# Retention with tokens as the stationary operand for v and the input norm applied behind the matmuls, and the first two units of two FFNs taken side by side

## The chip, the core and the metric

One core of one Trainium2 chip runs the whole program, a chain of eight phases over one sequence of 512 tokens. The metric is the device time of one execution in microseconds. The time before is the median of 3 runs.

## The reference, cut to what matters

x has 512 rows of 1024 numbers, all in float32. The first two of the eight phases are these (the fourth is the second one again with other weights):

```python
def retention(xn, w_in, w_out):              # xn = rms_norm(x, a_norm_pre)
    q, k, v, g = split(xn @ w_in)            # 1024 | 1024 | 2048 | 2048 columns, 4 heads
    q, k = rotary(q), rotary(k) * dk ** -0.5
    ...                                      # causal, with a decay per head:
    out = (q @ k.T * decay) @ v              # per head 512 x 512
    out = rms_norm(out)                      # over the 512 columns of a head
    return (silu(g) * out) @ w_out

def conv_ffn(xn, w_up, conv_w, conv_b, w_down):   # xn = rms_norm(x, gain)
    h = xn @ w_up                            # 1024 -> 5632
    hc = causal depthwise convolution of h, width 3
    g, u = split(hc)
    return (silu(g) * u) @ w_down
```

After each phase x = x + rms_norm(h, gain). The other phases (diff, conformer, nsa and two more FFNs) are not touched.

## The kernel before, in words

**Layout and precision.** x is kept transposed: 8 chunks of 128 features by 512 tokens. Every dense product works on split numbers: a value is a high part (`xh`, `w_hi`, rounded by a copy on ACT) and a low part (`xl`, `w_lo`, the difference). A product of a chunk is three matmuls of 512 columns: high by high, low by high, high by low (lines 720 to 722).

**A unit** is one 1024 x 128 slice of weights: 8 chunks, 24 matmuls, into one of two PSUM banks `lin`. Weights pass through two slots. SP loads `raw[s]` (line 540) as soon as the last `w_lo[s]` is made; ACT makes `w_hi[s]` (line 1266, `split`) once the slot's unit is multiplied (`unit_done`); DVE makes `w_lo[s]` (line 1819, `split_next`) and so sets `lo_done`, on which PE's unit after next waits. `bank_free` is set by whoever has read the bank. The order of work on each engine is the order in which the program is written; engines meet only at semaphores. `rounds` is a hardware loop.

**Opening.** ACT issues the DMAs for the constants, x, 37 pieces of parameters (`rows`) and `dif_lp` (lines 1768 to 1772). PE turns x into chunks (line 1206), DVE copies them to `x`, PE turns the parameters (line 1213). `norm_x` then squares each chunk on ACT (line 1274), sums over features with a matmul by ones into the bank `stat` (line 736), takes the logarithm and the exponential for the inverse rms (lines 1280 and 1282), scales x to `y` on DVE (1833), and makes `xh` on ACT (1303) and `xl` on POOL (651).

**Retention**, a loop over four heads of 12 units: two for q, two for k, four for v, four for the gate g. ACT copies each bank out (line 1366: `ret_raw`, or the silu of g into `ret_g`). DVE rotates q and k (1950 to 1954). Each 128 columns of v come out as features by tokens, so PE turns them (`turn_v`, line 773) and ACT places them (1378). Between gate units PE makes the scores (786) and, once DVE has multiplied them by the decay (1967), weighs v with them into the four banks `att` (794). ACT copies those to `ret_o` (1392), squares them, PE sums the squares (736), and DVE scales by the inverse rms and the gate (1976, 1978); `ret_hi` (1402) and `ret_lo` (1986) are the input of the last projection, `a_w_out`, in which each of 8 outputs takes two units, 16 chunks.

**ffn0 and ffn1.** The update of x before them ends on DVE chunk by chunk: y (1874), x (1877), `xl` (1838), with `xh` and a square on ACT (1288, 1274). PE's first unit takes for each chunk the sum of squares and the three matmuls, then unit 1 follows, then a loop of pairs of units. These FFNs multiply x times the gain without the rms; DVE multiplies each bank by the inverse rms `rs_x` (2400).

## Time and profile before

| | us |
|---|---|
| median of 3 runs | 3006.64 (3003.03 to 3008.56) |
| the profiled execution | 3006.15 |
| its span | 3004.3 |
| PE busy | 2822.2 (94%) |
| DVE busy | 1626.2 (54%) |
| ACT busy | 1215.4 (40%) |
| POOL busy | 192.1 (6%) |
| granted TensorE clock, mean | 0.969 |

The span runs from the first to the last instruction; the 1.85 us beside it in the execution's time lie around the program. Busy time of PE is that of pipelined matmuls whose ends are modelled, so one matmul is shown as 0.40 us where the next starts 0.23 us later. Starts are the safer reading.

### The profile page before, as it was taken

How to read it: one execution, taken by the hardware profiler on the slowest of the kernel's cores; microseconds unless marked ns; L12 is line 12 of the kernel's file. 1: busy time of each engine (PE TensorE's matmuls, PEld its weight loads, DVE VectorE, ACT ScalarE, POOL GpSimd, SP SyncE). 2: the span in 40 equal slices, each digit the busy share in tenths (PEclk: the TensorE clock that was granted, in tenths of full speed). 3: DMA queues.
4: the chain of work that ended last, by engine and by line, in shares of the span. 5: the costliest groups of instructions: out<-in, count | busy, mean ns of one | idle time of the engine just before them, and what ended most of it. 6: DMA issues, size and time to landing. Idle time of an engine off the chain costs nothing.

```text
span 3004.3 us, 34870 instructions
## 1 busy us (share of the span) xinstructions
PE 2822.2 (94%) x11902; PEld 2118.4 (71%) x11902; DVE 1626.2 (54%) x2216; ACT 1215.4 (40%) x1955; POOL 192.1 (6%) x173
## 2 busy tenths in 40 slices
PE   6999989999998998999988969999998898999999
PEld 4677757788886656888875637888876555678887
DVE  3234323777425674677436965555365667455533
ACT  3333322444324454444335654333234465443321
POOL 1000000000000000000005730000000112000000
PEclk8999989999999998999998979999998999999999
DMA  3122213233332211333331203333333000133332
GB/s 117 57 80 74 70 49 91 73 95 92 91 96 77 64 43 56 91 91 98 91 91 36 63 28 91 91 97 89 94 98 102 20 15 22 56 92 91 97 92 91
DMA packets 431346, 229.15 MB, mean 76 GB/s; under 512 B 7915, under 2 KB 427820, under 8 KB 431148
## 3 DMA queue, kind: packets, MB, share of 16 engines
q1 hardware_dynamic: 428848, 222.98, 25.5%
q10 hardware_dynamic: 2428, 5.28, 0.5%
q8 instruction: 39, 0.64, 0.1%
q14 instruction: 31, 0.25, 0.0%
HBM read 226.13 MB, written 2.10 MB: 76 GB/s over the span
## 4 chain that ended last, share of the span: by engine, by line
PE 81%; DVE 11%; ACT 4%; issue 2%; POOL 1%; ACTq 1%; DMA 0%; DVEq 0%; POOLq 0%; SPq 0%
PE lin L720 22%; PE lin L721 22%; PE lin L722 22%; DVE con_a L2238 2%; PE stat L736 2%; DVE w_lo L1819 2%; PE att L922 1%; PE lin L961 1%; PE att L794 1%; PE lin L984 1%; DVE n_sm L2147 1%; ACT w_hi L1266 1%; PE att L786 1%; PE lin L1138 1%; PE lin L1101 1%
## 5 line engine op out<-in xcount | busy, mean ns | idle before, releaser
L1819 DVE TENSOR_TENSOR w_lo<-raw,w_hi 128x1024 fp32r<-128x1024 f32 x427 | 527.6, 1236 | 775.9 <-ACT w_hi L1266 762.0
L720 PE MATMUL lin<-xh,w_hi 128*128 128x512 f32 x2048 | 830.8, 406 | 17.8 <-POOL xl L651 14.1
L721 PE MATMUL lin<-xl,w_hi 128*128 128x512 f32 x2048 | 813.7, 397 | 0.0
L722 PE MATMUL lin<-xh,w_lo 128*128 128x512 f32 x2048 | 813.4, 397 | 0.0
L1266 ACT ACTIVATE w_hi<-raw 128x1024 fp32r<-128x1024 f32 x427 | 452.1, 1059 | 665.4 <-PE lin L722 627.4
L720 PEld LDWEIGHTS lin<-xh,w_hi 128*128 128x128 f32 x2048 | 386.6, 189 | 131.5 <-issue 19.8
L721 PEld LDWEIGHTS lin<-xl,w_hi 128*128 128x128 f32 x2048 | 387.2, 189 | 97.2 <-issue 6.7
L722 PEld LDWEIGHTS lin<-xh,w_lo 128*128 128x128 f32 x2048 | 386.9, 189 | 95.0
L721 PE MATMUL lin<-ffn_lo,w_hi 128*128 128x512 f32 x704 | 279.1, 396 | 0.0
L720 PE MATMUL lin<-ffn_hi,w_hi 128*128 128x512 f32 x704 | 279.1, 396 | 0.0
L722 PE MATMUL lin<-ffn_hi,w_lo 128*128 128x512 f32 x704 | 279.1, 396 | 0.0
L720 PEld LDWEIGHTS lin<-ffn_hi,w_hi 128*128 128x128 f32 x704 | 132.6, 188 | 32.3
L722 PEld LDWEIGHTS lin<-ffn_hi,w_lo 128*128 128x128 f32 x704 | 132.6, 188 | 32.3
L721 PEld LDWEIGHTS lin<-ffn_lo,w_hi 128*128 128x128 f32 x704 | 132.6, 188 | 32.3
L1757 ACT ACTIVATE ffn_hi<-ffn_p 128x512 f32 x88 | 55.7, 633 | 218.2 <-DVE ffn_p L2423 130.5
L1755 ACT ACTIVATE ffn_s<-ffn_g 128x512 f32<-128x512 f32 x88 | 55.7, 633 | 184.2 <-DVE ffn_g L2411 184.2
L2400 DVE TENSOR_TENSOR ffn_hu<-lin,rs_x 128x512 f32<-128x512 f32 x88 | 60.8, 691 | 101.8 <-PE lin L722 101.7
L736 PE MATMUL stat<-sq,const 128*128 128x512 f32 x128 | 80.4, 751 | 36.3 <-ACT sq L1274 35.9
L657 POOL TENSOR_TENSOR x<-x,y 128x512 f32<-128x512 f32 x8 | 11.7, 1484 | 1524.2 <-DVE y L1874 1524.2
L2428 DVE TENSOR_TENSOR ffn_lo<-ffn_p,ffn_hi 128x512 f32 x88 | 60.9, 692 | 81.2 <-ACT ffn_hi L1757 81.2
L2400 DVE TENSOR_TENSOR ffn_hg<-lin,rs_x 128x512 f32<-128x512 f32 x88 | 60.9, 692 | 70.0 <-PE lin L722 40.9
L697 POOL TENSOR_SCALAR n_e<-n_e,n_sm,gates 128x128 f32<-128x128 f32 (+1 forms) x64 | 50.1, 782 | 738.5 <-DVE n_sm L2153 738.5
(328 smaller groups left out, 3562.6 us busy)
## 6 DMA issues: line engine op xcount, KB each, us to landing
raw<-in_ffn_w_up SPq DMA_DIRECT2D x176, 512.0 KB, 3.8
raw<-in_ffn_w_down SPq DMA_DIRECT2D x64, 512.0 KB, 3.7
raw<-in_a_w_in SPq DMA_DIRECT2D x48, 512.0 KB, 3.9
raw<-in_ffn_w_down SPq DMA_DIRECT2D x32, 384.0 KB, 3.2
raw<-in_conv_w_pw SPq DMA_DIRECT2D x24, 512.0 KB, 3.8
raw<-in_nsa_w_in SPq DMA_DIRECT2D x21, 512.0 KB, 3.8
raw<-in_a_w_out SPq DMA_DIRECT2D x16, 512.0 KB, 3.7
raw<-in_w_kv SPq DMA_DIRECT2D x16, 512.0 KB, 3.7
```

The costliest lines, as they stand in the source:

```text
L697: pool.tensor_scalar(n_e[:, sl, 1, 0:w], n_e[:, sl, 1, 0:w], n_inv[:, sl, 1:2], gate, ALU.mult, ALU.mult).then_inc(n_b, 1)
L720: pe.matmul(bank, w_hi[s][:, k, :], h, start=start and k == 0, stop=False)
L721: pe.matmul(bank, w_hi[s][:, k, :], l, start=False, stop=False)
L722: done = pe.matmul(bank, w_lo[s][:, k, :], h, start=False, stop=stop and k == kc - 1)
L736: pe.matmul(stat[:, :], c_("ones"), sq[(squares.n - 1) % 2][:, :], start=start, stop=stop).then_inc(sq_used, 1)
L1266: act.activation(w_hi[s][:, :, :], raw[s][:, :, :], ACT.Copy).then_inc(hi_done[s], 1)
L1755: act.activation(ffn_s[:, :], ffn_g[:, :], ACT.Silu).then_inc(f_silu, 1)
L1757: act.activation(ffn_hi[:, bass.ds(i, 1), :], ffn_p[:, :], ACT.Copy).then_inc(f_hi, 1)
L1819: dve.tensor_tensor(w_lo[s][:, :, :], raw[s][:, :, :], w_hi[s][:, :, :].bitcast(F32), ALU.subtract).then_inc(lo_done[s], 1)
L2238: done = dve.scalar_tensor_tensor(part[:, k:], att[:, 3, 0:T - k], col("conv_w_dw_2", c + j * DC), part[:, k:], ALU.mult, ALU.add)
L2400: dve.tensor_tensor(ffn_h[u][:, :], lin[b][:, :], rs_x[:, :], ALU.mult).then_inc(f_h[u], 1)
L2428: dve.tensor_tensor(ffn_lo[:, bass.ds(i, 1), :], ffn_p[:, :], ffn_hi[:, bass.ds(i, 1), :].bitcast(F32), ALU.subtract).then_inc(f_lo, 1)
```

## The change

**The norm.** a_norm_pre's gain is loaded by itself and turned into `gain_cols`. `xh` and `xl` are made from x times the gain; the inverse rms of the tokens (`ret_rs`) is applied later: to the rotation tables for q and k, to each gate bank on DVE before the silu, and to v as a scale per token (`ret_rc`, `ret_rs` turned by PE). x is loaded in two halves. PE takes the first two units side by side, chunk by chunk, with the turns of x and the sums of squares between them. The parameter rows, `ret_tab` and `dif_lp` are issued by SP behind the first two weight loads, and PE turns the parameters behind units 1 and 2.

**v.** A v unit is now 256 rows by 512 columns of weights: x's tokens are the stationary operand, the weights move, and v comes out tokens by features in `att`.

**The heads** are written out instead of looped. ACT squares `att` itself, DVE adds the squares to `acc`, and PE sums once per head. a_w_out's first product waits for one piece of `ret_lo` at a time.

**ffn0 and ffn1** take units 0 and 1 side by side, unit 1 four chunks behind; ACT splits unit 0's slot before it loads the silu table, and the first pair stands ahead of the loop.

The core of the diff, by engine:

```diff
@@ -548,10 +560,22 @@

             def retention():
...
-                            load(w_cols(w, 0, UC, h * width + (base_ + c * P)))
+                for h in range(RH):
+                    for n in range(4):
+                        load(w_cols(w, 0, UC, h * RDK + (n // 2) * RH * RDK + (n % 2) * P))
+                        if h == 0 and n == 1:
+                            for dst, src in row_dmas(a, rows):
+                                sp.dma_start(dst, src).then_inc(rows_in, 16)
+                            sp.dma_start(ret_tab[:, :], a["ret_table"]).then_inc(r_tab, 16)
+                            sp.dma_start(dif_lp, a["b_lambda"][0].rearrange("r c -> (r c)").partition_broadcast(P)).then_inc(d_lp, 16)
+                    for u in range(4):
+                        s, t = units.take()
+                        sp.wait_ge(lo_done[s], t + 1)
+                        sp.sem_inc(slot_taken, 1)
+                        sp.dma_start(broad(raw[s]), w[u * 2 * P:(u + 1) * 2 * P, 2 * RH * RDK + h * RDV:2 * RH * RDK + (h + 1) * RDV].rearrange(
+                            "(c p) n -> p c n", p=P)).then_inc(raw_full[s], 16)
+                    for c in range(RC):
+                        load(w_cols(w, 0, UC, 2 * RH * RDK + RH * RDV + h * RDV + c * P))
                 project(a["a_w_out"][0], (8, 8), DC)

```

PE:

```diff
             def retention():
-                xs = norm_x()
-                vt, vd, gs = Tally(), Tally(), Tally()
-                with rounds(pe, RH, (units, 12), (banks, 12), (squares, RC), (heads, 1), (vt, RC), (vd, RC),
-                            (r_scores, TB), (r_outs, RC)):
...
+                two = [(units.take(), banks.take()) for _ in range(2)]
...
+                for c in range(DC + 3):
+                    if 4 + c < DC:
+                        turn_x(4 + c)
+                    if c < DC:
+                        chunk(0, c)
+                        sum_square(c == 0, c == DC - 1)
+                    if c >= 3:
+                        chunk(1, c - 3)
...
+                def values(h):
+
+                    for u in range(4):
+                        s, t = units.take()
+                        pe.wait_ge(lo_done[s], t + 2)
+                        if h and u == 0:
+                            pe.wait_ge(r_og, h * RC)
+                        for c in range(2):
+                            k = 2 * u + c
+                            for b in range(TB):
+                                tok = slice(b * P, (b + 1) * P)
+                                pe.matmul(att[:, b, :], xh[:, k, tok], broad(w_hi[s])[:, c, :], start=k == 0, stop=False)
+                                pe.matmul(att[:, b, :], xl[:, k, tok], broad(w_hi[s])[:, c, :], start=False, stop=False)
+                                done = pe.matmul(att[:, b, :], xh[:, k, tok], broad(w_lo[s])[:, c, :], start=False, stop=k == DC - 1)
+                        done.then_inc(unit_done[s], 1)
...
+                for h in range(RH):
+                    if h:
+                        output(xh, xl, (UC,))
+                        output(xh, xl, (UC,))
+                    else:
+                        pe.wait_ge(rows_in, ROW_DMAS * 16)
+                        pe.wait_ge(gain_set, 1)
+                        turn_params(0, 4)
+                    output(xh, xl, (UC,))
+                    if h == 0:
+                        pe.wait_ge(par_done, 1)
+                        turn_params(4, PARAM_TILES)
+                    output(xh, xl, (UC,))
+                    if h == 0:
+                        pe.wait_ge(par_done, 2)
+                        pe.wait_ge(r_rms, 1)
...
                     output(xh, xl, (UC,))
+                    output(xh, xl, (UC,))
                     for c in range(RC):
-                        sum_square(c == 0, c == RC - 1)
-                    for c in range(RC):
-                        vd.next(), r_scores.next(), r_outs.next()
-                project(ret_hi, ret_lo, (8, 8), DC, lambda k: (r_lo, (RH * RC)))
+                        squares.next()
+                    pe.wait_ge(sq_used, squares.last())
+                    pe.matmul(stat[:, :], c_("ones"), acc[:, :], start=True, stop=True).then_inc(r_sum, 1)
+                project(ret_hi, ret_lo, (8, 8), DC, lambda k: (r_lo, k + 1))
                 sum_acc()
...
+                else:
+                    two = [(units.take(), banks.take()) for _ in range(2)]
...
+                    for c in range(DC + LAG):
+                        if c < DC:
+                            sum_square(c == 0, c == DC - 1)
+                            chunk(0, c)
+                        if c >= LAG:
+                            chunk(1, c - LAG)
...
+            pe.wait_ge(gain_in, 16)
+            pe.transpose(trp[:, 0, 0:DC], gain_rows[:, :], c_("ident")[0:DC, 0:DC]).then_inc(gain_tr, 1)
+            for c in range(4):
+                turn_x(c)
```

ACT:

```diff
             def retention(final):
-                norm_x()
-                with rounds(act, RH, (units, 12), (banks, 12), (squares, RC), (rss, 1), (heads, 1)) as i:
...
+                act.preload_act_table_set(LN)
+                for c in range(DC):
+                    act.wait_ge(x_ready, c + 1)
+                    act.activation(xh[:, c, :], x[:, c, :], ACT.Copy, scale=gain_cols[:, c:c + 1]).then_inc(xh_ready, 1)
+                    pre.next()
+                    square(x[:, c, :])
...
+                def gate(h, c):
+
+                    split_next()
+                    banks.take()
+                    act.wait_ge(r_gr, h * RC + c + 1)
+                    act.activation(ret_g[:, c, :], ret_g[:, c, :], ACT.Silu).then_inc(r_g, 1)
+
+                for h in range(RH):
+                    if h:
+                        act.wait_ge(r_pv, h * RC)
+                    raw_out(ret_raw[:, 0, :])
+                    raw_out(ret_raw[:, 1, :])
...
+                    act.wait_ge(r_rot, 2 * h + 1)
+                    raw_out(ret_raw[:, 0, :])
...
+                        split_next()
+                    s, t = multiplied()
+                    for b in range(TB):
+                        act.activation(ret_v[:, b, :], att[:, b, :], ACT.Copy, scale=ret_rc[:, b:b + 1]).then_inc(r_v, 1)
+                    split(s, t)
+                    gate(h, 0)
+                    gate(h, 1)
...
+                        act.wait_ge(r_pv, h * RC + c + 1)
+                        square(att[:, c, :])
+                    gate(h, 2)
+                    gate(h, 3)
+                    act.preload_act_table_set(LN)
...
+                    if h + 1 < RH:
+                        act.preload_act_table_set(SILU)
                     for c in range(RC):
...
+                        act.wait_ge(r_p, h * RC + c + 1)
+                        act.activation(ret_hi[:, h * RC + c, :], y[c % 2][:, :], ACT.Copy).then_inc(r_hi, 1)
+                project_out(ret_hT, 2, final, ("ffn_norm_pre", 0), table=False)
...
+                if kind == 1:
+                    split_next()
...
+                if kind == 1:
+                    pair(0, False)
+                with rounds(act, FC - (kind == 1), (units, 2), (banks, 2), (f_n, 1)) as i:
+                    pair(i + (kind == 1), True)
```

DVE (and POOL, which no longer makes xl in this phase):

```diff
+                def gate(h, c):
+
+                    b, _t = banks.take()
+                    s, t = units.n % 2, units.base + units.n // 2
+                    dve.wait_ge(unit_done[s], t + 1)
+                    dve.tensor_tensor(ret_g[:, c, :], lin[b][:, :], ret_rs[:, :], ALU.mult).then_inc(r_gr, 1)
+                    dve.wait_ge(r_gr, h * RC + c + 1)
+                    dve.sem_inc(bank_free[b], 1)
+                    split_next()
...
+                    if h == 0:
+                        dve.wait_ge(rs_ready, rss.next())
+                        dve.wait_ge(r_tab, 16)
+                        dve.tensor_tensor(cos, cos, ret_rs[:, :], ALU.mult).then_inc(r_scaled, 1)
+                        dve.tensor_tensor(sin, sin, ret_rs[:, :], ALU.mult).then_inc(r_scaled, 1)
+                        dve.wait_ge(r_scaled, 2)
+                    rotate(ret_q, 2 * h)
...
+                    for u in range(4):
+                        split_next()
+                    gate(h, 0)
+                    for j in range(TB):
+                        dve.wait_ge(r_s, h * TB + j + 1)
+                        dve.tensor_tensor(ret_s[j], att[:, j, 0:T - j * P], ret_tab[:, (2 + h) * T:(3 + h) * T - j * P], ALU.mult).then_inc(r_sd, 1)
+                    gate(h, 1)
+                    first_, second = squares.next(), squares.next()
+                    dve.wait_ge(sq_ready, second)
+                    dve.tensor_tensor(acc[:, :], sq[0][:, :], sq[1][:, :], ALU.add).then_inc(sq_used, 2)
+                    add_square()
+                    add_square()
+                    gate(h, 2)
+                    gate(h, 3)
+                    for c in range(RC):
+                        dve.wait_ge(r_g, h * RC + c + 1)
+                        dve.tensor_tensor(ret_g[:, c, :], att[:, c, :], ret_g[:, c, :], ALU.mult).then_inc(r_og, 1)
                     dve.wait_ge(rs_ready, rss.next())
-                    for _ in range(RC):
-                        squares.next()
                     for c in range(RC):
+                        dve.wait_ge(r_og, h * RC + c + 1)
                         if c >= 2:
-                            dve.wait_ge(r_lo, (h - 1) * RC + c - 1)
-                        dve.tensor_tensor(y[c % 2][:, :], ret_o[:, c, :], rs[:, :], ALU.mult).then_inc(r_p, 1)
-                        dve.wait_ge(r_p, (h - 1) * 2 * RC + 2 * c + 1)
-                        dve.tensor_tensor(y[c % 2][:, :], y[c % 2][:, :], ret_g[:, c, :], ALU.mult).then_inc(r_p, 1)
+                            dve.wait_ge(r_lo, h * RC + c - 1)
+                        dve.tensor_tensor(y[c % 2][:, :], ret_g[:, c, :], rs[:, :], ALU.mult).then_inc(r_p, 1)
                         if c:
...
+            def first_low(c):
+                dve.wait_ge(xh_ready, pre.next())
+                dve.scalar_tensor_tensor(xl[:, c, :], x[:, c, :], gain_cols[:, c:c + 1], xh[:, c, :].bitcast(F32),
+                                         ALU.mult, ALU.subtract).then_inc(xl_ready, 1)
+
             for c in range(DC):
                 dve.wait_ge(tr_done, c + 1)
                 dve.tensor_copy(x[:, c, :], att[:, c % 4, :]).then_inc(x_ready, 1)
+                if c:
+                    first_low(c - 1)
+            first_low(DC - 1)
```

The order moves at three places. The first is PE in the opening. Before (`sq` to `stat` are the sums of squares, `trp` the parameter turns):

```order
L1213 MATMUL trp<-const,rows 128x128 x3
L1213 MATMUL trp<-const,rows 128x128 [waits par_done]
L1213 MATMUL trp<-const,rows 128x128 x2
L1213 MATMUL trp<-const,rows 128x69
L736 MATMUL stat<-sq,const 128x512 [waits sq_ready] x8
L109 UNCONDITIONAL_BRANCH
L109 ISA
L713 REGISTER_ALU [waits bank_free0]
L720 MATMUL lin<-xh,w_hi 128x512 [waits xl_ready,lo_done0]
L721 MATMUL lin<-xl,w_hi 128x512
L722 MATMUL lin<-xh,w_lo 128x512
```

and now (`att` is x being turned, L810 to L812 one chunk of unit 0):

```order
L788 MATMUL att<-const,x_in 128x128 x3
L788 MATMUL att<-const,x_in 128x128 [waits x_ready,x_landed1]
L788 MATMUL att<-const,x_in 128x128 x3
L810 MATMUL lin<-xh,w_hi 128x512 [waits xl_ready,bank_free0,lo_done0]
L811 MATMUL lin<-xl,w_hi 128x512
L812 MATMUL lin<-xh,w_lo 128x512
L760 MATMUL stat<-sq,const 128x512 [waits sq_ready]
L788 MATMUL att<-const,x_in 128x128 [waits x_ready,x_landed1]
L788 MATMUL att<-const,x_in 128x128 x3
```

All eight sums stood ahead of the first product; now a turn of x, a chunk and a sum alternate. The second is ACT at the end of head 0; before, from the last squares to the first `ret_hi`:

```order
L1274 ACTIVATE sq<-ret_o 128x512 [waits sq_used]
L1271 REGISTER_ALU [waits r_o]
L1274 ACTIVATE sq<-ret_o 128x512 [waits sq_used]
L1398 REGISTER_ALU
L1280 ACTIVATE log_ms<-stat,eps 128x512 [waits sq_used]
L1281 REGISTER_ALU
L1282 ACTIVATE rs<-log_ms 128x512 [waits ln_done]
L1401 ISA
L1402 ISA [waits r_p]
L1402 ACTIVATE ret_hi<-y 128x512
```

and now, from the third gate unit to the next head's first raw copy:

```order
L1355 ACTIVATE w_hi<-raw 128x1024 [waits raw_full0,unit_done0]
L1470 ACTIVATE ret_g<-ret_g 128x512 [waits r_gr]
L1355 ACTIVATE w_hi<-raw 128x1024 [waits raw_full1,unit_done1]
L1470 ACTIVATE ret_g<-ret_g 128x512 [waits r_gr]
L1509 ACT_TABLE_LOAD
L1369 ACTIVATE log_ms<-stat,eps 128x512 [waits r_sum]
L1371 ACTIVATE rs<-log_ms 128x512 [waits ln_done]
L1514 ACTIVATE dif_sm<-dif_sm 128x2 [waits d_lam]
L1516 ACT_TABLE_LOAD
L1519 ACTIVATE ret_hi<-y 128x512 [waits r_p] x4
L1460 ACTIVATE ret_raw<-lin 128x512 [waits unit_done0,r_pv]
```

The squares left this stretch (they stand behind the weighing of v), and a second table load stands ahead of `ret_hi`. The third is PE at ffn0's fifth chunk. Before:

```order
L736 MATMUL stat<-sq,const 128x512 [waits sq_ready]
L720 MATMUL lin<-xh,w_hi 128x512 [waits xl_ready]
L721 MATMUL lin<-xl,w_hi 128x512
L722 MATMUL lin<-xh,w_lo 128x512
L736 MATMUL stat<-sq,const 128x512 [waits sq_ready]
```

and now (L1278 to L1280, once for each unit):

```order
L760 MATMUL stat<-sq,const 128x512 [waits sq_ready]
L1278 MATMUL lin<-xh,w_hi 128x512 [waits xl_ready]
L1279 MATMUL lin<-xl,w_hi 128x512
L1280 MATMUL lin<-xh,w_lo 128x512
L1278 MATMUL lin<-xh,w_hi 128x512 [waits xl_ready]
L1279 MATMUL lin<-xl,w_hi 128x512
L1280 MATMUL lin<-xh,w_lo 128x512
```

A chunk of unit 1 has come in behind each chunk of unit 0.

## Rows read from the trace of the kernel before

**Rows 1.** The page, part 4: shares of the chain that ended last, by engine.
```profile
PE 81%; DVE 11%; ACT 4%; issue 2%; POOL 1%; ACTq 1%; DMA 0%; DVEq 0%; POOLq 0%; SPq 0%
```

**Rows 2.** PE's waits, 0 to 549 us: who waited for whom, total, times, longest.
```profile
PE stat L736 <- ACT sq L1274: 21.7, 6, 4.4
...
PE lin L720 <- DVE ret_lo L1986: 10.0, 1, 10.0
...
PE lin L720 <- DVE w_lo L1819: 1.8, 3, 0.6
```

**Rows 3.** Windows: start:end, length, busy time of each engine (instructions), PEclk, DMA share, GB/s.
```profile
38.80:50.00 11.20, 8.75 (x18) 5.16 (x18) 7.59 (x8) 3.78 (x6) 7.33 (x7) 0.51 0.00 0
149.20:241.00 91.80, 87.64 (x361) 65.55 (x361) 32.19 (x40) 31.60 (x46) 0.00 (x0) 0.98 0.24 69
422.60:515.50 92.90, 92.90 (x384) 74.24 (x384) 22.96 (x23) 23.10 (x30) 0.00 (x0) 0.97 0.29 84
527.80:545.00 17.20, 16.76 (x60) 10.51 (x59) 12.66 (x19) 10.61 (x15) 0.00 (x0) 1.00 0.00 1
549.00:700.00 151.00, 151.00 (x649) 121.31 (x648) 109.12 (x136) 65.90 (x81) 0.00 (x0) 1.00 0.32 94
```

**Rows 4.** Timeline of the opening: start us, length us, engine, line, operation, count.
```profile
17.74 2.00 ACT L1775 ACTIVATE w_hi<-raw 128x1024 fp32r<-128x1024 f32 x2
...
23.88 10.50 PE L736 MATMUL stat<-sq,const 128*128 128x512 f32 x16 [2.99 <-ACT sq L1274]
...
44.97 2.50 POOL L651 TENSOR_TENSOR xl<-y,xh 128x512 fp32r<-128x512 f32 x2 [1.29 <-ACT xh L1303]
...
52.13 0.40 PE L720 MATMUL lin<-xh,w_hi 128*128 128x512 f32 x1
```

**Rows 5.** DMA issues: the first load (with its us to landing), the first seven loads.
```profile
raw<-in_a_w_in SPq DMA_DIRECT2D x1, 512.0 KB, 9.7
...
DMA to landing us min/median/max: 3.7/4.0/12.8
```

**Rows 6.** The chain in head 1: start us, us, engine, tile, line, count.
```profile
171.84 0.44 PE trp L773 x4
...
223.67 5.54 PE stat L736 x8
```

**Rows 7.** Timeline of the boundary from head 1 to head 2, PE, ACT and DVE.
```profile
220.63 1.05 ACT L1266 ACTIVATE w_hi<-raw 128x1024 fp32r<-128x1024 f32 x1
221.69 1.28 ACT L1394 ACT_TABLE_LOAD   x1
...
223.67 5.52 PE L736 MATMUL stat<-sq,const 128*128 128x512 f32 x8 [3.57 <-ACT sq L1274]
...
230.62 0.69 DVE L1976 TENSOR_TENSOR y<-ret_o,rs 128x512 f32<-128x512 f32 x1 [7.68 <-ACT rs L1282]
...
239.70 1.23 DVE L1819 TENSOR_TENSOR w_lo<-raw,w_hi 128x1024 fp32r<-128x1024 f32 x1 [0.62 <-ACT w_hi L1266]
```

**Rows 8.** Timeline of PE at the start of a_w_out.
```profile
422.58 0.77 PE L720 MATMUL lin<-ret_hi,w_hi 128*128 128x512 f32 x1 [10.02 <-DVE ret_lo L1986]
```

**Rows 9.** Timeline of ffn0's first unit.
```profile
534.90 0.50 PE L720 MATMUL lin<-xh,w_hi 128*128 128x512 f32 x1 [0.22 <-DVE xl L1838]
...
536.15 0.74 DVE L1838 SCALAR_TENSOR_TENSOR xl<-x,params,xh 128x512 fp32r<-128x512 f32 x1
...
536.95 0.50 PE L720 MATMUL lin<-xh,w_hi 128*128 128x512 f32 x1 [0.22 <-DVE xl L1838]
```

**Rows 10.** The chain at ffn1's start.
```profile
1190.39 1.71 PE stat L736 x2
...
1196.47 0.86 PE stat L736 x2
...
1198.03 0.86 PE stat L736 x2
```

**Rows 11.** Window of PE in the diff phase's v units, columns as above.
```profile
921.00:933.00 12.00, 12.00 (x53) 1.00 0.15 44
```

293 lines of the change are left out of this document (148 added, 145 removed).

## The prediction

> **What bounds the kernel now.** The chain of waits comes first: 81% of the span lies on PE [rows 1], so time is won only where PE stands idle, does work that can go, or runs at the lower clock. PE's waits up to 549 us name those places: 21.7 us for the squares of ACT, 10.0 us for ret_lo, 1.8 us in three pieces for w_lo [rows 2]. The windows by stage give the yardstick [rows 3]: 649 matmuls of 512 columns in 151.00 us, 0.2327 us each, so a chunk (three matmuls) is 0.70 us and a unit (24) 5.58 us at clock 1.00, the 2.4 GHz level. One head takes 91.80 us, of which 12 units are 67.0. At clock 0.51 (1.2 GHz, 38.80 to 50.00 us) all of this costs nearly twice as much: a sum of squares is a pair of matmuls of 1.71 us there and 0.86 at the full clock [rows 10].
>
> **Part 1, the opening and the first two units.** Before [rows 4], ACT issues 40 DMAs and splits the first weights at 17.74; then the norm runs as a series: squares from 23.88, the inverse rms, then y, xh, xl chunk by chunk, POOL's xl at 1.25 us each. Unit 1 starts at 52.13 and ends 5.58 later, at 57.7. The change takes the rms out: chunk products start on x times the gain. What ends last now is the second weight load. The first load, issued at 1.1, landed 9.7 us later, at 10.8; the second, issued near 1.8, took the longest of all, 12.8 us: it landed at 14.6 [rows 5]; and DVE now splits it before it copies x. With the parameter rows moved behind it on SP I expect 12.0 us; the bounds are those two, 10.8 and 14.6. Then w_hi 1.05, w_lo 1.23, the copy of x 0.69 (as DVE's other passes of 512 columns), xh 0.7, xl 0.74, with hops 4.7 us [rows 7, 9]: the first chunk at 16.7 us. PE's work is 16 chunks (11.2), 8 sums (6.9) and 3 more turns of x (3 x 0.44 = 1.3): 19.4 us, above the 8 x 1.5 us in which ACT and DVE feed it. The lower clock lasted some 4 to 6 us after the other starts (in ffn1 the pair of 1190.39 still took 1.71 us, that of 1196.47 took 0.86 [rows 10]); it costs half of that, so I add 2.5 us: end at 38.6. Gain 57.7 - 38.6 = 19.1. Against it PE now turns the parameters (twice) and the rms (once) between units: 3 x 0.44 = 1.3. Net **17.8 us**. Hidden: 37 row DMAs, ret_tab and the lambda load stand ahead of unit 2's load on SP, some 16 us of issuing; that load is wanted near 35 us. If SP were 15 us later it would show one for one. ret_tab is first wanted near 42 us, before at 58.
>
> **Part 2, one head.** Removed from PE: 16 transposes of v, 4 x 0.44 = 1.8 us [rows 6]; the wait for squares, 3.57; eight stat matmuls, 5.54, of which one pair stays, 0.86. The v units keep 96 matmuls with x stationary and w moving; the same form in the diff phase runs 53 matmuls in 12.00 us [rows 11], so nothing is added. ACT drops four copies to ret_v and four to ret_o and adds four copies with the token's rms as a scale. These stand ahead of a split: 4 x 0.6 + 1.05 + 1.23 + 0.2 = 4.9 us, hidden under a unit of 5.58 with 0.7 to spare. The gate product on DVE (0.69) and the silu behind it are hidden too. The acc sums (3 x 0.69) lie under the gate units; where they were late, PE's single stat pair would wait.
>
> The head boundary [rows 7]: before, PE's third unit waited 0.6 us for w_lo. Now both sides get shorter. PE frees at 0 and has 0.86 + 2 x 5.58 = 12.0 us to do. ACT and DVE: unit seen 0.2, w_hi 1.05, w_lo 1.23, four products att x gate 2.8, then eight operations y and ret_lo 5.5 and hops 0.5: 11.3, ACT's last ret_hi at 10.5; then raw copy 0.6, w_hi 1.05, w_lo 1.23, hops: 13.6. So PE waits 1.6 us, 1.0 more than before. The table loads (1.28 each) end before the products do. Per boundary 1.8 + 3.6 + 4.7 - 1.0 = 9.1; I take **9.0, three times: 27.0 us**. Bounds per boundary: 10.5 (no wait at all) and 7.5 (1.5 us more).
>
> **Part 3, last head into a_w_out.** Here 1.8 + 3.6 + 4.7 us again, and the wait of 10.02 us for all of ret_lo [rows 8] goes: PE now asks for one piece at a time, and the last head's four are pieces 12 to 15, reached 0.86 + 12 x 0.70 = 9.3 us after the gate unit. They come at 7.7, 9.2, 10.6 and 11.4, against 9.3, 10.0, 10.7 and 11.4: hidden to within 0.1. The projection took 92.90 us for 384 matmuls [rows 3], 89.4 at the full clock; started without a pause it keeps that, 3.5 gained (one start at the lower clock, so I count 3.3). Next late is its third weight piece, 0.9 us, since ACT splits it after ret_hi. Sum **22.5 us**; bounds 18.5 (the clock penalty stays and 0.5 us is lost) and 23.4.
>
> **Part 4, ffn0 and ffn1 side by side.** In ffn0 PE ran at DVE's pace for chunks 4 to 6, 2.05 us apart [rows 9], with 1.56 us of work each: some 1.3 us idle. Filled with unit 1's chunks a step is 2.26 us and PE the bound: unit 1 ends about **1.1 us** earlier. In ffn1 the steps were 1.56 apart already (1196.47, 1198.03 [rows 10]): **0**. The new risk is unit 2: after the last square it needs logarithm, exponential, w_hi and w_lo, 0.7 + 0.63 + 1.05 + 1.23 + hops = 4.0 us, and PE has 6 chunks, 4.2 us. Bounds per layer -1.0 and +1.3.
>
> **Sum.** 17.8 + 27.0 + 22.5 + 1.1 = 68.4 us. From the profiled execution's 3006.15 us (span 3004.3) that is 2937.75; the median of the runs is 0.5 higher: 2938 us.
>
> **A rule against it.** PE now alternates between two lin banks and stat in the opening and in ffn0, ffn1, and the v units go round four att banks. The trace has both habits: at 527.80 to 545.00 PE alternates between stat and lin at clock 1.00, and the diff phase's rotation runs at clock 1.00 too [rows 3, 11]. The Trainium skill, "TensorE: Matmul & The Clock Gate", section "A second HAM failure mode: psum-queue depth-cycling", says that going round PSUM banks makes PE idle for moments and its clock swing between the levels. By this trace the rule does not bind here: by the rows the sum is 2938 us, and were the low clock to stay in those places it would be 2953 to 3042 us (rivals 1 and 3).
>
> **Rivals.**
> 1. The opening stays at 1.2 GHz, as 38.80 to 50.00 did [rows 3], because feeding is ragged. Then 19.4 us of work costs about 36.5: 15 us more, 2953. For: the old opening did that. Against: then PE was starved by a chain through POOL (1.25 us a chunk) that is gone, and its work per chunk now exceeds the feed.
> 2. Small waits come in: the boundary chain 1.5 us longer three times, the v copies 1 us late in four heads, the second load at 14.6 instead of 12.0: 6 to 11 us, about 2946. For: ACT and DVE carry out everything in order, with 0.7 us spare. Against: each link above has a measured duration.
> 3. Slower than before: the bank rotation holds PE at 1.2 GHz in all v units. 16 units x 5.58 = 89 us and the opening 15 more: 2938 + 104 = 3042. It decides once more than 68 of those 104 us are lost, two thirds of the rotation at the low clock. Against: the diff phase's v units at clock 1.00 [rows 11]. The section of the Trainium skill named above would give this rival.
> 4. The side-by-side part does nothing, as supply never binds once PE starts slowly: 2939, inside the forecast's own range.
>
> **Chances.** Forecast (with rival 4) 0.70, rival 1 0.10, rival 2 0.18, rival 3 0.02. The forecast's own range is 2931 to 2944: the bounds of the opening (+1.2, -2.6) and of three boundaries (+-4.5) carry it. To leave out no more than 2 in 10 it must reach over most of rivals 1 and 2: 2930 to 2955. A measurement of this kernel can tell about 0.2% (6 us) from no change. Faster by more: 0.97; within: 0.01; slower: 0.02.
>
> **What would show it.** Right: first lin matmul near 17 us, unit 1's end near 39 and clock 1.00 from about 22; heads of 82 to 83 us; stat pairs without a wait for squares; wait for ret_lo below 0.5 us; the projection in 90 us; ffn0's second unit ending 19.8 us after its first stat instead of 20.9. Wrong: wait time on w_lo after the v units or over 3 us at a boundary, clock below 0.9 in the v units, or the first chunk later than 20 us. The step I trust least is the landing of the second load; it is worth 3 us. The forecast falls if the total gain is below 50 us.

## The result and the profile after

| | before | after |
|---|---|---|
| median, us | 3006.63 (4 runs) | 2930.14 (4 runs, 2928.99 to 2931.54) |
| the profiled execution, span | 3004.3 | 2928.8 |
| PE busy | 2822.2 | 2786.8 |
| granted TensorE clock, mean | 0.969 | 0.976 |

The ratio is 0.9748, 95% interval 0.9736 to 0.9760: 76.5 us faster, where 68.4 were forecast. The time lies 0.14 us inside the lower edge of the range (2930), less than its own four runs are apart (two of them lie below 2930), and just below the forecast's own range of 2931 to 2944. The page's chain shares:

```profile
PE 83%; DVE 11%; ACT 4%; issue 1%; POOL 1%; DMA 1%; DVEq 0%; ACTq 0%; POOLq 0%; SPq 0%
```

PE's waits from 0 to 480 us, after (who waited for whom: total, times, longest), against [rows 2]:

```profile
PE trp L1302 <- DMA const<-in_const: 6.3, 1, 6.3
PE att L788 <- DMA x_in<-in_x: 4.4, 1, 4.4
PE stat L760 <- ACT sq L1363: 4.3, 1, 4.3
PE stat L780 <- DVE acc L1966: 3.0, 1, 3.0
PE lin L744 <- DVE w_lo L1939: 2.2, 4, 0.7
```

The four heads' waits for squares and the 10.0 us for ret_lo are gone. The third row is ffn0's start, the fourth the sum at the end of retention; both stood before too. Windows by stage, after (columns as in [rows 3]): units 0 and 1, head 0 to head 1, the projection, the update, ffn0's first two units:

```profile
15.29:34.71 19.42, 19.42 (x80) 13.24 (x78) 9.00 (x13) 8.99 (x14) 0.00 (x0) 1.00 0.46 142
75.41:157.33 81.92, 81.23 (x340) 62.50 (x339) 36.75 (x47) 27.73 (x37) 0.00 (x0) 1.00 0.26 78
351.00:441.70 90.70, 90.40 (x386) 72.20 (x384) 32.30 (x37) 29.01 (x38) 0.00 (x0) 1.00 0.31 91
441.70:451.30 9.60, 2.35 (x4) 0.42 (x2) 4.58 (x7) 4.57 (x7) 0.00 (x0) 0.68 0.25 74
451.30:471.40 20.10, 20.03 (x64) 13.10 (x65) 15.47 (x23) 12.64 (x20) 0.00 (x0) 0.90 0.00 0
```

The opening, after (timeline: start, length, engine, line):

```profile
9.87 1.06 ACT L1901 ACTIVATE w_hi<-raw 128x1024 fp32r<-128x1024 f32 x1 [2.16 <-DMA raw<-in_a_w_in]
...
10.99 4.55 PE L788 MATMUL att<-const,x_in 128*128 128x128 f32 x20 [4.44 <-DMA x_in<-in_x]
12.14 0.69 DVE L2608 COPY x<-att 128x512 f32<-128x512 f32 x1
12.87 0.73 ACT L1450 ACTIVATE xh<-x,gain_cols 128x512 fp32r<-128x512 f32 x1 [0.65 <-DVE x L2608]
...
13.62 0.75 DVE L2603 SCALAR_TENSOR_TENSOR xl<-x,gain_cols,xh 128x512 fp32r<-128x512 f32 x1
...
15.29 0.48 PE L810 MATMUL lin<-xh,w_hi 128*128 128x512 f32 x1
...
34.71 0.60 PE L795 MATMUL trp<-const,rows 128*128 128x128 f32 x4
```

The first chunk starts at 15.29, and the clock is full from that chunk on. Its xl was made by 14.37: what ended last was PE itself, with the 20 turns of x that stand ahead of the chunk. Units 0 and 1 end at 34.71, 19.42 us later: the 19.4 us of work of the prediction, with nothing beside it. The boundary of head 0 (of all engines; PE from the answer for PE alone):

```profile
104.99 1.02 PE L881 MATMUL stat<-acc,const 128*128 128x512 f32 x2
...
107.42 2.48 DVE L2122 TENSOR_TENSOR ret_g<-att,ret_g 128x512 f32<-128x512 f32 x4
...
115.44 1.05 ACT L1355 ACTIVATE w_hi<-raw 128x1024 fp32r<-128x1024 f32 x1
116.52 1.22 DVE L1939 TENSOR_TENSOR w_lo<-raw,w_hi 128x1024 fp32r<-128x1024 f32 x1 [0.74 <-ACT w_hi L1355]
...
117.89 0.47 PE L744 MATMUL lin<-xh,w_hi 128*128 128x512 f32 x1 [0.69 <-DVE w_lo L1939]
```

The sum runs at once, and PE's only wait is 0.69 us for the third unit's w_lo.

**Where the 75.5 us of span come from**, by starts of the same operation in both traces:

| stretch | forecast | measured |
|---|---|---|
| opening, to the fifth unit: unit 1's end 57.7 to 34.71, less the turns now between units | 17.8 | 21.7 |
| three head periods, 91.54, 91.81, 91.68 to 81.92, 81.81, 81.82 | 27.0 | 29.5 |
| last head, projection and update, to ffn0's first sum (total 72.7 by there) | 22.5 | 21.5 |
| ffn0's first sum to its unit 2, 20.87 to 20.06; ffn1's, 21.06 to 21.07 | 1.1 | 0.8 |
| from there on, in stages that no edit touches | 0 | 2.0 |

### The profile page after: what moved, and what is told of

Same layout as the page of the kernel before. It is cut to its first block, busy times and chain, and to the rows that moved or that the text cites. A ratio compares the mean times of both kernels' runs of the same rounds, so it can differ in the third digit from the quotient of the medians.

```text
span 2928.8 us, 34258 instructions
## 1 busy us (share of the span) xinstructions
PE 2786.8 (95%) x11819; PEld 2101.6 (72%) x11819; DVE 1642.2 (56%) x2246; ACT 1196.6 (41%) x1924; POOL 182.1 (6%) x165
## 4 chain that ended last, share of the span: by engine, by line
PE 83%; DVE 11%; ACT 4%; issue 1%; POOL 1%; DMA 1%; DVEq 0%; ACTq 0%; POOLq 0%; SPq 0%
PE lin L744 21%; PE lin L745 21%; PE lin L746 21%; DVE con_a L2384 2%; DVE w_lo L1939 2%; PE stat L760 2%; PE att L1002 1%; PE lin L1041 1%; PE att L873 1%; PE att L837 1%; PE att L838 1%; PE att L836 1%; ACT w_hi L1355 1%; PE lin L1064 1%; DVE n_sm L2293 1%
## 5 line engine op out<-in xcount | busy, mean ns | idle before, releaser
L744 PE MATMUL lin<-xh,w_hi 128*128 128x512 f32 x1872 | 751.4, 401 | 10.1 <-POOL xl L675 6.8
L745 PE MATMUL lin<-xl,w_hi 128*128 128x512 f32 x1872 | 742.4, 397 | 0.0
L746 PE MATMUL lin<-xh,w_lo 128*128 128x512 f32 x1872 | 742.3, 397 | 0.0
L744 PEld LDWEIGHTS lin<-xh,w_hi 128*128 128x128 f32 x1872 | 352.7, 188 | 106.6 <-issue 15.0
L745 PEld LDWEIGHTS lin<-xl,w_hi 128*128 128x128 f32 x1872 | 353.0, 189 | 87.6 <-issue 3.6
L746 PEld LDWEIGHTS lin<-xh,w_lo 128*128 128x128 f32 x1872 | 352.8, 188 | 86.2
L744 PE MATMUL lin<-ffn_hi,w_hi 128*128 128x512 f32 x704 | 279.1, 396 | 0.0
L744 PEld LDWEIGHTS lin<-ffn_hi,w_hi 128*128 128x128 f32 x704 | 132.6, 188 | 32.3
L1876 ACT ACTIVATE ffn_hi<-ffn_p 128x512 f32 (+1 forms) x88 | 55.6, 632 | 218.3 <-DVE ffn_p L2569 130.6
L2574 DVE TENSOR_TENSOR ffn_lo<-ffn_p,ffn_hi 128x512 f32 (+1 forms) x88 | 60.9, 693 | 81.6 <-ACT ffn_hi L1876 81.6
L708 POOL TENSOR_TENSOR con_p<-con_p,con_x 128x512 f32<-128x512 f32 x64 | 89.7, 1402 | 9.2
```

Source lines behind the costliest of these rows:

```text
L708: pool.tensor_tensor(con_p[:, c % 2, :], first_, con_x[:, k % 4, :], ALU.add).then_inc(c_pool, 1)
L744: pe.matmul(bank, w_hi[s][:, k, :], h, start=start and k == 0, stop=False)
L745: pe.matmul(bank, w_hi[s][:, k, :], l, start=False, stop=False)
L746: done = pe.matmul(bank, w_lo[s][:, k, :], h, start=False, stop=stop and k == kc - 1)
L1876: act.activation(ffn_hi[:, at(i), :], ffn_p[:, :], ACT.Copy).then_inc(f_hi, 1)
L2574: dve.tensor_tensor(ffn_lo[:, at(i), :], ffn_p[:, :], ffn_hi[:, at(i), :].bitcast(F32), ALU.subtract).then_inc(f_lo, 1)
```

## The experiments

Times are compared with the changed kernel (2930.14 us), unless another is named; each ratio is to the kernel before, which ran beside each of the three groups (medians 3005.47, 3003.95 and 3005.75).

**1. Side by side undone.**

```diff
-LAG = 4
+LAG = 8
-                for c in range(DC + 3):
+                for c in range(DC + 8):
-                    if c >= 3:
-                        chunk(1, c - 3)
+                    if c >= 8:
+                        chunk(1, c - 8)
```

> Undoes the side-by-side order alone, in all three places: unit 1 starts only when unit 0 has all its chunks (lag 8 instead of 3 in the opening, 8 instead of 4 in ffn0 and ffn1); everything else as in the changed kernel. Theory (supply hardly binds): in the opening a step of unit 0 with its turn and its sum is 2.0 us of PE's own work for the first four chunks, so unit 1 ends 0.4 to 0.8 us later than 34.71; in ffn0 unit 2 starts 20.9 us behind the first sum instead of 20.06; in ffn1 21.0 as before. Whole kernel +1.5 us, 2931.5. Rival (the side-by-side order is what feeds PE in the opening): unit 1's end moves by 3 us or more, and PE's waits name xl.

Measured: 2931.38 us, ratio 0.9756 (0.9740 to 0.9773). PE in the opening and in ffn0 (timelines; L744 is unit 2):

```profile
15.04 0.48 PE L810 MATMUL lin<-xh,w_hi 128*128 128x512 f32 x1
...
34.50 0.60 PE L795 MATMUL trp<-const,rows 128*128 128x128 f32 x4
...
451.21 2.08 PE L760 MATMUL stat<-sq,const 128*128 128x512 f32 x2 [4.31 <-ACT sq L1363]
...
472.16 0.39 PE L744 MATMUL lin<-xh,w_hi 128*128 128x512 f32 x1
```

In the opening the two units take 19.46 us one after the other and 19.42 side by side: the order is worth nothing there, the expected 0.4 to 0.8 us do not appear, and the rival falls. From the first sum to unit 2, ffn0 takes 20.95 against 20.06 us, worth 0.9. In ffn1 it is 20.96 (1114.35 to 1135.31), which against the first trace's 21.07 looks like nothing; but the ten later traces of kernels with the pairing, the control of experiment 9 among them, take 19.93 to 19.96 there, so the pairing is worth 1.0 us in ffn1 too. The whole kernel is 1.2 us slower, less than the runs can tell. The opening's pairing was never what won its time.

**2. The projection waits for all of ret_lo again.**

```diff
-                project(ret_hi, ret_lo, (8, 8), DC, lambda k: (r_lo, k + 1))
+                project(ret_hi, ret_lo, (8, 8), DC, lambda k: (r_lo, RH * RC))
```

> Undoes one wait: every chunk of the first a_w_out outputs waits for all sixteen pieces of ret_lo again. Theory: the projection starts at 361.8 instead of 350.99 (+10.8), and its first products run at 1.2 GHz after the idle time, as they did before the change, 2.5 to 3.3 us more: +13.5 us, 2943.6. Rival (the wait by pieces only moves the idle time to piece 12): the projection starts later but ends less than 4 us later, total under 2935.

Measured: 2942.24 us, ratio 0.9791 (0.9775 to 0.9808), 12.1 us slower. PE's timeline there:

```profile
361.75 0.76 PE L744 MATMUL lin<-ret_hi,w_hi 128*128 128x512 f32 x1 [9.61 <-DVE ret_lo L2081]
...
367.83 0.40 PE L746 MATMUL lin<-ret_hi,w_lo 128*128 128x512 f32 x1
```

The wait is 9.61 us, and for the 6.1 us behind it products start 0.43 us apart instead of 0.23: fourteen of them, 2.8 us. Both terms of Part 3 stand, the second with 2.8 us where 3.3 were counted.

**3. Squares behind the last gate unit.**

```diff
+                    gate(h, 2)
+                    gate(h, 3)
                     for c in range(RC):
                         act.wait_ge(r_pv, h * RC + c + 1)
                         square(att[:, c, :])
-                    gate(h, 2)
-                    gate(h, 3)
```

and DVE's additions behind its gates 2 and 3 likewise.

> Puts the four squares and their sums behind the last gate unit of each head again, still added up by DVE with a single sum on PE. Theory: PE's sum then waits for w_hi 1.05, silu 0.6, the table load 1.28, four squares and the last addition, about 6.6 us, in each of four heads; the next head's 0.7 us wait for w_lo goes, and PE's start at the lower clock costs 1 to 2 us more: 7.4 a head, about +28 us, 2958. Head period 81.8 becomes 89. Rival (the sum of the squares was never on the path once the third unit's weights are what ends last): period under 84, total under 2938.

Measured: 2959.07 us, ratio 0.9839 (0.9823 to 0.9856), 28.9 us slower. PE's waits, and the timeline at head 0's end:

```profile
PE stat L881 <- DVE acc L1966: 22.6, 4, 5.7
```

```profile
110.48 2.08 PE L881 MATMUL stat<-acc,const 128*128 128x512 f32 x2 [5.65 <-DVE acc L1966]
111.56 1.42 PE L744 MATMUL lin<-xh,w_hi 128*128 128x512 f32 x1
...
116.57 0.39 PE L745 MATMUL lin<-xl,w_hi 128*128 128x512 f32 x1
```

Of some 7.3 us a head 5.65 are the wait and the rest is mostly the low clock: the next ten products, until 116.57, start 0.43 us apart and more; the granted clock from the sum to there is 0.51 (1.2 GHz). So the place of the squares ahead of gates 2 and 3 is the largest single item of Part 2. The 7.3 us are its price in the changed kernel, not what the kernel before lost by it: there the wait was 3.57 us [rows 7], and DVE had no squares to add up ahead of PE's sums.

**4. PE sums the squares.**

```diff
-                    output(xh, xl, (UC,))
-                    output(xh, xl, (UC,))
...
-                    pe.matmul(stat[:, :], c_("ones"), acc[:, :], start=True, stop=True).then_inc(r_sum, 1)
+                    for c in range(0, RC, 2):
+                        output(xh, xl, (UC,))
+                        sum_square(c == 0, False)
+                        v = squares.next()
+                        pe.wait_ge(sq_ready, v)
+                        done = pe.matmul(stat[:, :], c_("ones"), sq[(squares.n - 1) % 2][:, :], start=False, stop=c == RC - 2)
+                        done.then_inc(sq_used, 1)
```

> Lets PE sum the four squares of a head again (two behind each of the last two gate units, without a wait, since the squares are early), instead of DVE's additions and one sum. Theory: six more matmuls of 0.43 us a head, 2.6 us; behind the last unit PE has 1.7 us of sums instead of 0.86, so its 0.7 us wait for w_lo at the boundary goes: +1.9 for three heads, +2.6 for the last, +8.3 us, 2938.5; head period 83.7. Rival (the boundary is bound by ACT and DVE anyway): the period grows by under 1 us.

Measured: 2936.97 us, ratio 0.9771 (0.9755 to 0.9787), 6.8 us slower. From the first to the last scores of the four heads it is 254.9 us instead of 249.8, 1.7 us a head, and the wait for w_lo at the boundaries is gone from the waits. PE's free 0.7 us took part of the added 2.6, as expected.

**5. Parameter DMAs back on ACT.**

```diff
-                            for dst, src in row_dmas(a, rows):
-                                sp.dma_start(dst, src).then_inc(rows_in, 16)
...
+            for dst, src in row_dmas(a, rows):
+                act.dma_start(dst, src).then_inc(rows_in, 16)
             act.wait_ge(gain_tr, 1)
```

> Puts the 37 parameter DMAs back on ACT, behind x and ahead of the first splits of weights; SP issues only ret_tab and the lambda load behind the first two weights. Theory: ACT issues for 12 to 15 us more, so the first w_hi comes at 16 to 17.7 instead of 6.66 and the first chunk at 21 to 23.5 instead of 15.29 (+6 to +8); by then PE has stood idle for 8 us behind its first turns of x, so the clock is at 1.2 GHz for about 6 us of work and costs 2.5 us more: unit 1's end 43 to 46, whole kernel about 2940. Rival (the clock does not depend on what PE did before the first chunk): same first chunk, steps of 2.0 us from the start, unit 1's end 41 to 43, whole kernel about 2937.

Measured: 2944.79 us, ratio 0.9803 (0.9788 to 0.9818), 14.7 us slower. ACT and PE in its opening:

```profile
22.26 1.99 ACT L1901 ACTIVATE w_hi<-raw 128x1024 fp32r<-128x1024 f32 x2
...
26.45 1.09 PE L786 MATMUL att<-const,x_in 128*128 128x128 f32 x4 [8.20 <-DVE x L2608]
...
28.00 0.77 PE L808 MATMUL lin<-xh,w_hi 128*128 128x512 f32 x1 [0.46 <-DVE xl L2603]
```

and its windows from the first chunk to unit 1's end:

```profile
28.00:34.00 6.00, 6.00 (x17) 3.92 (x18) 4.33 (x7) 2.71 (x6) 0.00 (x0) 0.64 0.27 76
34.00:49.46 15.46, 15.46 (x61) 10.61 (x60) 5.44 (x7) 7.04 (x11) 0.00 (x0) 1.00 0.00 0
```

The first chunk comes 12.7 us later, not 6 to 8: ACT spends 18.0 us on 37 DMAs (2.87 to 20.87), and its first split stands behind all of them. In the changed kernel SP spends 14.4 us on them (2.03 to 16.5), and in the kernel before ACT itself did (1.63 to 16.03): ACT is not the slower issuer. Most of the other 3.6 us lie in the three pieces of ffn_conv_w, first in the kernel before, then here:

```profile
4.74 1.32 ACTq L1771 DMA_DIRECT2D rows<-in_ffn_conv_w  x3
...
5.60 4.76 ACTq L1896 DMA_DIRECT2D rows<-in_ffn_conv_w  x3
```

No run shows why these three took longer here. Then the clock: 21.46 us for work that takes 19.42, so idle time ahead of the chunk costs 2.04 us.

**6. The same, with PE kept busy.**

```diff
+            pe.wait_ge(gain_set, 1)
+            for n in range(28):
+                pe.transpose(trp[:, n % 4, :], const[:, (n % 5) * P:(n % 5 + 1) * P], c_("ident"))
             if run[0]:
```

> The kernel with the parameter DMAs on ACT, and 28 transposes of constants on PE that nobody reads, behind the gain's turn, in the time in which PE would stand idle ahead of the first chunk. Theory (the turns ahead of the first chunk are what brought the full clock): they run from about 16 to 20 or 21, the first chunk comes at the same time as without them, the clock is at full speed within 2 us of it, and unit 1 ends 1.5 to 2.5 us earlier than without them. Rival: unit 1's end is the same or later.

Measured: 2943.14 us, ratio 0.9795 (0.9780 to 0.9810). Its windows:

```profile
28.24:34.00 5.76, 5.76 (x26) 3.77 (x26) 4.97 (x8) 3.84 (x7) 0.00 (x0) 1.00 0.27 77
34.00:47.66 13.66, 13.66 (x55) 9.48 (x54) 4.79 (x7) 5.92 (x9) 0.00 (x0) 1.00 0.01 1
```

19.42 us again, with clock 1.00 from the first chunk. The transposes ran from 22.66 us to the first chunk's last turn at 27.74, not from about 16, because they wait for the gain's copy on ACT. That settles the term of 2.5 us in Part 1: the clock of the first chunks hangs on what PE did just before, and in the changed kernel the 20 turns of x that reach up to 15.5 us did it.

**7. Idle time of the updates filled.**

```diff
+            def warm(n):
+                for _ in range(n):
+                    pe.matmul(trp[:, :, :].rearrange("p b n -> p (b n)"), c_("ones"), const[:, 0:T], start=True, stop=True)
...
-                sum_acc()
+                sum_acc(3, 4)
```

(three ahead of the sum, four behind it, at the end of retention, ffn0, diff and ffn1).

> Adds products that nobody reads (ones times constants, into the idle bank trp) to the changed kernel: three pairs ahead of the sum at the end of retention, ffn0, diff and ffn1, four pairs behind it, where PE stands idle for 3.0 and 4.3 us. Theory (idle time costs the clock, and the clock costs the first products behind it): the sum's pair takes 1.1 instead of 1.99 us, and ffn0's and ffn1's first chunks 1.56 instead of 3.1 us: 2 us at the end of retention, 3 at ffn1's start, 1 to 2 at the other two, about 7 in all, 2923. Rival (the added pairs run at the low clock themselves, 1.71 us each, and delay the sum or the first chunk): 2 to 4 us slower at each of the four places, 2938 or more.

Measured: 2926.47 us, ratio 0.9737 (0.9724 to 0.9750), 3.7 us faster than the changed kernel. ffn1's start in the changed kernel:

```profile
1111.41 2.08 PE L760 MATMUL stat<-sq,const 128*128 128x512 f32 x2 [4.31 <-ACT sq L1363]
...
1114.56 1.91 PE L760 MATMUL stat<-sq,const 128*128 128x512 f32 x2
...
1132.48 0.39 PE L744 MATMUL lin<-xh,w_hi 128*128 128x512 f32 x1
```

and in this one:

```profile
1102.69 2.74 PE L777 MATMUL trp<-const 128*128 128x512 f32 x6
1105.86 1.12 PE L785 MATMUL stat<-acc,const 128*128 128x512 f32 x2 [0.43 <-DVE acc L1972]
1106.82 3.60 PE L777 MATMUL trp<-const 128*128 128x512 f32 x8
1111.30 1.12 PE L760 MATMUL stat<-sq,const 128*128 128x512 f32 x2 [0.89 <-ACT sq L1369]
```

The low clock is gone, but only half of the 7 us is won. The stretch from the first sum to unit 2 is 19.93 us instead of 21.07, because PE at full speed now waits for DVE's xl (0.22 us a chunk, 2.05 us apart, as in [rows 9]). Yet the control, the same kernel without added products, takes 19.95 there, though its first sum ran at the low clock:

```profile
1111.80 2.07 PE L760 MATMUL stat<-sq,const 128*128 128x512 f32 x2 [4.31 <-ACT sq L1363]
...
1131.75 0.39 PE L744 MATMUL lin<-xh,w_hi 128*128 128x512 f32 x1
```

So the added products win nothing in that stretch: behind a short spell of low clock PE catches up with DVE's pace anyway, and 21.07 is what the first trace alone lost with two chunks at the low clock. Below the clock lay the supply. By the end of ffn1 this trace is 1.2 us ahead of the changed kernel's first and 1.5 ahead of the control (table below). The rest arises behind it, between the ends of ffn1 and nsa, where only the four pairs behind ffn1's sum are added: 1056.0 us here, 1057.5 in the control, and 1054.9 to 1059.2 in all kernels without added products. Where the rest of the gain comes from stays open.

**8. A shorter opening.** x in four pieces of 512 KB; w_hi and w_lo of unit 1 behind the first chunks; PE's chunk ahead of its next turn:

```diff
-                    if 4 + c < DC:
-                        turn_x(4 + c)
                     if c < DC:
                         chunk(0, c)
+                    if 4 + c < DC:
+                        turn_x(4 + c)
+                    if c < DC:
                         sum_square(c == 0, c == DC - 1)
```

> Shortens the opening further: x comes in four pieces of 512 KB instead of two of 1 MB; ACT loads its table ahead of the second weight split and makes w_hi of unit 1 behind xh of chunk 0; DVE makes unit 1's w_lo behind the third copy of x; PE takes a chunk ahead of the next turn of x. Theory: the first chunk waited for x's first half (10.99) and, through the fifth turn that stood ahead of it on PE, for the second half. With the first 512 KB landed near 9 the first chunk comes at 12.5 to 13.5 instead of 15.29, and since PE has 19.4 us of work from there, unit 1 ends 2 to 2.8 us earlier: 2927.7. Rival (DMA traffic of 350 GB/s sets the pace, and later pieces of x starve PE): first chunk earlier, unit 1's end within 0.5 us of 34.71, 2930.

Measured: 2929.06 us, ratio 0.9742 (0.9729 to 0.9756): from the changed kernel not to be told apart by the median. In the trace:

```profile
9.53 3.68 PE L788 MATMUL att<-const,x_in 128*128 128x128 f32 x16 [3.15 <-DMA x_in<-in_x]
13.06 0.76 PE L810 MATMUL lin<-xh,w_hi 128*128 128x512 f32 x1
13.62 0.63 PE L811 MATMUL lin<-xl,w_hi 128*128 128x512 f32 x1
```

The first chunk comes 2.2 us earlier, but with fewer turns ahead of it it starts at the low clock (0.56 us to the next start), and unit 1's end, 33.38, is only 1.3 us earlier: less than the theory's 2 to 2.8, more than the rival's 0.5. The work that took 19.42 us takes 20.32. About half of these 0.9 us is the clock of the first chunk (1.26 us for three products, where the changed kernel took 0.79); the last kernel below, at the full clock from its first chunk, still takes 20.25, since DVE's w_lo of unit 1 now stands ahead of xl (from 15.35 us there, and PE's third chunk waits until 17.88).

**9 to 11. A control, both edits together, and the conformer paired too.** The last one's added edit:

```diff
-                for c in range(DC):
-                    output(xh, xl, (UC,), xs)
-                    output(xh, xl, (UC,))
+                for c in range(DC + LAG):
+                    if c < DC:
+                        chunk(0, c)
+                    if c >= LAG:
+                        chunk(1, c - LAG)
```

(for its first two units alone), and 14 transposes of constants ahead of the first turn of x.

> The changed kernel itself, unedited, run again beside the next two. Both theories expect its 2930 us within 3; its trace shows how far the phases that no edit touches move between two executions: theory, the opening and the four heads repeat within 0.5 us, and the diff and nsa phases differ by 0.6 to 3 us in steps, as they did between the runs so far. Rival: all phases repeat within 0.5 us, and the 2.2 us that the diff phase gained in the first trace of the changed kernel belong to the change.

> The shorter opening and the added products of the two kernels before it together. Theory: the gains lie at different places and add, 1.3 and about 3.5 us: 2925 to 2926. Rival: the added products' gain was luck with the phases that vary, total 2929.

> The same, with 14 transposes of constants ahead of the first turns of x, and the conformer's first two units side by side too, unit 1 four chunks behind. Theory: the opening gets back the 0.9 us that its first chunks lost to the low clock; in the conformer PE waits for POOL's xl, 1.9 us a chunk for 0.70 to 1.28 us of work, so four chunks of unit 1 fit in, and 2.8 us of unit 1 stay behind unit 0: 3 to 4 us less; total 2921 to 2922. Rival (unit 2 of the conformer then waits for its weights, 3 us behind unit 0's end, and takes the gain back): total 2925, with a wait for w_lo there.

Measured: control 2930.22 us, ratio 0.9749 (0.9735 to 0.9762); both 2924.90, 0.9730 (0.9717 to 0.9743), as the theory has it, and each of its five runs is faster than each of the control's, so the gain of the two edits together is not luck; with the conformer 2921.98, **0.9724 (0.9711 to 0.9737), the fastest of all**, 8.2 us below the control. In the conformer, unit 2 started 20.67 us behind the first chunk in the changed kernel's first trace (1517.70 to 1538.37), 20.48 in the control and 20.23 in the kernel with both edits; in the last kernel 17.74:

```profile
1513.36 0.77 PE L1132 MATMUL lin<-xh,w_hi 128*128 128x512 f32 x1 [4.33 <-POOL xl L675]
...
1531.10 0.40 PE L744 MATMUL lin<-xh,w_hi 128*128 128x512 f32 x1
```

2.5 us less than in the kernel that differs from it by this edit and the 14 transposes alone, 2.7 to 2.9 less than in the others, where 3 to 4 were expected; the rival's wait for w_lo does not appear. The 14 transposes brought nothing: the clock was full from the first chunk (0.31 us to the next start), but that chunk came at 13.49 instead of 13.06, and unit 1's end at 33.74 instead of 33.38.

The control answers how far untouched stages move. Starts of the same logarithm on ACT, each less that of the changed kernel's first trace:

| at the end of | before | experiment 1 | experiment 7 | control |
|---|---|---|---|---|
| retention (447.10) | +72.58 | -0.16 | -0.37 | -0.06 |
| ffn0 (834.84) | +74.24 | +1.51 | -0.65 | +0.08 |
| diff (1107.13) | +75.57 | +2.94 | -0.11 | +0.39 |
| ffn1 (1495.72) | +75.65 | +2.82 | -1.24 | +0.21 |
| nsa (2554.64) | +75.54 | -0.10 | -4.17 | -1.24 |

At these marks the same kernel repeats within 0.4 us up to ffn1 and moves by 1.5 from there to the end of nsa; between the marks ffn1's start moved by 1.1 (21.07 and 19.95) and its closing sum by 0.9 the other way; kernels whose stages start at other times gain or lose up to 3 us in code they share. Half of the theory fell: diff repeats. One place shows the grain, the sum at the end of each phase, always behind 3.0 us of idle time. Before, at the end of retention and of ffn0 (at that of diff and ffn1 it took 2.08 and 1.13):

```profile
518.51 1.13 PE L756 MATMUL stat<-acc,const 128*128 128x512 f32 x2 [3.01 <-DVE acc L1846]
...
906.97 2.07 PE L756 MATMUL stat<-acc,const 128*128 128x512 f32 x2 [3.01 <-DVE acc L1846]
```

After, the same two:

```profile
445.07 1.99 PE L780 MATMUL stat<-acc,const 128*128 128x512 f32 x2 [3.01 <-DVE acc L1966]
...
833.50 1.30 PE L780 MATMUL stat<-acc,const 128*128 128x512 f32 x2 [3.01 <-DVE acc L1966]
```

The same operation after the same idle time costs from 1.1 to 2.1 us.

## Why the prediction was right, and where its sizes were off

**Direction and main mechanisms** were right; the four parts came to 73.5 us against 68.4, and 2.0 us more came from outside them. That the median still lies inside the range, by 0.14 us, is luck: the gain was 8.1 us above the forecast, and the terms below say where.

**Part 1 (17.8, measured 21.7).** Two terms were mis-sized. The first chunk came at 15.29, not 16.7. The second weight load landed at 9.87, before the 10.8 that I took as its earliest. By my chain from the last load to xl the chunk could then have started at 14.4, where xl was ready; what ended last was a path that I had left out, x's first half at 10.99 and then PE's own turns of x: 16 in 3.7 us, and four more from 14.70 that stand ahead of the chunk. And the 2.5 us for the low clock were not paid, since the turns of x run into the first chunk; I took [rows 10], where PE had idled, for a place where it had not. Experiments 5 and 6 put 2.04 us on it. The sum 11.2 + 6.9 + 1.3 = 19.4 held to 0.02 us. I had named the move of the 37 DMAs only for its cost on SP, as hidden; its gain stood in the sum without a price of its own, and it is a large piece: undone in the changed kernel, it costs 12.7 us of start and 2.0 of clock, 14.7 us, where unit 1's end moved by 23.0. Some 3.6 of the 14.7 are issuing on ACT that was slower in experiment 5 than in the kernel before (18.0 and 14.4 us), so the move itself won less than 14.7. The norm put behind the matmuls, and POOL taken out of the chain, share the rest; the runs do not part them.

**Part 2 (9.0 a boundary, measured 9.8).** The predicted wait of 1.6 us was 0.7. DVE's four products in a row took 2.48 us, 0.62 each, where I had taken 0.7, and the chain from PE's last gate unit to the third unit's start was 12.9 us instead of 13.6. Experiments 3 and 4 price the two halves in the changed kernel: 7.3 us a head for the squares' place, 1.7 for the six sums. With the 1.8 us of transposes that is more than the 9.8 measured: such prices do not add up to what the change won.

**Part 3 (22.5, measured 21.5).** The wait and the clock behind it stand (9.61 us, and 2.8 where I had counted 3.3, in experiment 2). The third weight piece was 0.3 us late, not 0.9. Lost instead were 0.9 us at the closing sum, which ran at the low clock this time (1.99 instead of 1.13 us).

**Part 4 (1.1 and 0, measured 0.8 and 0 in the first trace).** Right for ffn0 (0.9 in experiment 1). For ffn1 the 0 held only in that trace. I had read from [rows 10] that PE's steps of 1.56 us were the pace there; they were PE catching up behind two chunks at the low clock. Where one chunk alone ran at it, as in experiment 1, PE waited for DVE's xl (0.17 to 0.22 us a chunk, 2.05 us apart), and the pairing took that away: 20.96 to 19.95 us, worth 1.0.

**Not in the sum:** 2.0 us in stages that the change does not touch. Of them 0.8 are ffn0's closing sum (2.07 and 1.30 us); 1.3 arose from there to the end of diff, a stretch of shared code that took 272.3 us in this trace and 271.2 to 274.5 in the others.

**Rivals.** 1 (opening at 1.2 GHz) and 3 (rotation of banks) fell: clock 1.00 in the opening and in every head. The rule of the Trainium skill weighed against the change, "TensorE: Matmul & The Clock Gate", section "A second HAM failure mode: psum-queue depth-cycling", does not bind here: with the v units going round four banks a head runs at 1.00. 2 (small waits) came out the other way: the waits at the boundary and at the third weight piece were shorter than forecast. 4 is right for the opening (experiment 1) and wrong for the FFNs, where the pairing is worth 0.9 and 1.0 us.

## What to carry to other kernels

Count what an engine issues, not only what it computes: 37 small DMAs put back ahead of ACT's first split cost 14.7 us, more than any reordering of the opening. Before pairing two streams to fill gaps, compare PE's own work per step with the supply per step at the clock that it really runs at; where the work is larger, pairing wins nothing. Read that step from more than one trace: ffn1's start gave 21.07 us once and 19.95 ten times. And here a wait of 5.7 to 9.6 us on PE cost its length and some 2 to 3 us of low clock behind it (the waits of 0.7 us at the boundaries cost no clock), so a wait by pieces, or squares taken two units earlier, returns more than the wait.
